# Gathering expert 0's rows turned, with the tokens as stationary operand, in a decoder layer with 32 experts

## What is computed

```python
def moe_ffn(h, w_router, b_router, w1, b1, w2, b2):
    logits = h @ w_router + b_router
    top_logit, top_e = lax.top_k(logits, 4)
    gate = softmax(top_logit)
    # for each expert e, over the tokens tok that chose it:
    #   u = h[tok] @ w1[e] + b1[e]          (1024 -> 2048: gate and linear half)
    #   y = clamped_swiglu(u) @ w2[e] + b2[e]   (1024 -> 1024)
    #   out[tok] += y * g

x = x + dot(concatenate([ret, moba]), w_out)
x = x + moe_ffn(rms_norm(x, norm2_w), ...)
out = rms_norm(x, final_norm_w)
```

## Time and profile before

| | |
|---|---|
| time, median of 3 runs | 1038.68 us (1038.46 to 1039.01) |
| the profiled execution: time, and its span from first to last instruction | 1039.17 us, 1037.3 us |
| PE busy | 1020.7 us (98%), 4880 matmul instructions |
| PEld, DVE, ACT busy | 409.8, 245.4, 126.5 us |
| mean granted PE clock | 0.997 |
| DMA | 424.64 MB, mean 409 GB/s |
| chain that ended last | PE 90%, DMA 7%, SPq 1% |

### The profile page before, as it was taken

One profiled execution on the slowest core, in us unless ns is written; L12 is line 12 of the kernel. 1 busy time (PEld: TensorE's weight loads), 2 busy tenths in 40 slices (PEclk: granted clock), 3 DMA queues, 4 the chain that ended last, 5 costly groups with the idle time before them and its releaser, 6 DMA issues.

```text
span 1037.3 us, 11270 instructions
## 1 busy us (share of the span) xinstructions
PE 1020.7 (98%) x4880; PEld 409.8 (40%) x4880; DVE 245.4 (24%) x610; ACT 126.5 (12%) x246; POOL 0.2 (0%) x4
## 2 busy tenths in 40 slices
PE   9999999999999999999999999999999999999996
PEld 8888433333333333333333333333333333333331
DVE  5776332111111111111111111111111111111111
ACT  2433120000000000000000000000000000000002
POOL 0000000000000000000000000000000000000000
PEclk9999999999999999999999999999999999999999
DMA  9983999999999999999999999999999999999995
GB/s 324 365 337 143 418 376 425 426 428 426 434 432 426 438 429 427 435 427 429 434 429 433 430 428 437 429 428 435 426 432 433 429 430 433 428 436 420 430 421 227
DMA packets 36104, 424.64 MB, mean 409 GB/s; under 512 B 3176, under 2 KB 16112, under 8 KB 19536
## 3 DMA queue, kind: packets, MB, share of 16 engines
q1 hardware_dynamic: 35744, 423.51, 97.0%
q10 hardware_dynamic: 304, 0.33, 0.1%
HBM read 422.78 MB, written 1.05 MB: 409 GB/s over the span
## 4 chain that ended last, share of the span: by engine, by line
PE 90%; DMA 7%; SPq 1%; DVE 0%; another core or an unknown queue 0%; issue 0%; ACT 0%; DVEq 0%
PE PS L1837 40%; PE PS L1860 19%; DMA ring<-in_w 7%; PE PS L1442 6%; PE PS L1806 5%; PE PS L1788 5%; PE PS L1685 3%; PE PS L1645 3%; PE PS L1895 2%; PE PS L1798 2%; PE PS L1411 1%; PE PS L1780 1%; SPq L543 1%; PE PS L1388 0%; PE PS L1968 0%; PE PS L1982 0%
## 5 line engine op out<-in xcount | busy, mean ns | idle before, releaser
L1837 PE MATMUL PS<-ring,work 128*64 128x512 f32 x1976 | 433.8, 596 | 6.0 <-DMA ring<-in_w 5.5
L1837 PEld LDWEIGHTS PS<-ring,work 128*64 128x64 f32 x1976 | 139.6, 137 | 277.2 <-issue 266.5
L1860 PE MATMUL PS<-ring,work 128*64 128x512 f32 x1024 | 227.9, 596 | 0.9 <-DMA ring<-in_w 0.8
L1860 PEld LDWEIGHTS PS<-ring,work 128*64 128x64 f32 x1024 | 72.0, 137 | 153.8 <-issue 148.9
L1300 DVE TENSOR_SCALAR work<-PS 128x512 f32<-128x512 f32 x32 | 22.1, 691 | 385.4 <-PE PS L1837 385.4
L841 ACT ACTIVATE work<-work 128x512 f32<-128x512 f32 x32 | 20.2, 631 | 523.5 <-DVE work L1300 523.5
L1265 DVE TENSOR_TENSOR work<-PS,n2w 128x512 f32<-128x512 f32 x30 | 20.7, 691 | 228.5 <-PE PS L1798 228.5
L1442 PE MATMUL PS<-ring 128*128 128x256 f32 x280 | 64.5, 382 | 0.0
L1806 PE MATMUL PS<-late,work 64*128 64x512 f32 x248 | 61.9, 616 | 0.0
L1788 PE MATMUL PS<-resid,work 128*64 128x512 f32 x248 | 58.5, 592 | 0.0
L1442 PEld LDWEIGHTS PS<-ring 128*128 128x128 f32 x280 | 51.7, 190 | 7.7 <-issue 1.4
(11 more groups left out here) (196 smaller groups left out, 453.2 us busy)
## 6 DMA issues: line engine op xcount, KB each, us to landing
ring<-in_w SPq DMA_DIRECT2D x72, 4096.0 KB, 34.8
ring<-in_w SPq DMA_DIRECT2D x35, 2048.0 KB, 13.5
ring<-in_w SPq DMA_DIRECT2D x22, 1024.0 KB, 8.4
ring<-in_w_in SPq DMA_DIRECT2D x11, 1024.0 KB, 12.1
ring<-in_w_out SPq DMA_DIRECT2D x4, 1024.0 KB, 11.1
ring<-in_w SPq DMA_DIRECT2D x6, 512.0 KB, 7.0
ring<-in_w_in SPq DMA_DIRECT2D x2, 512.0 KB, 5.8
work<-in_w SPq DMA_DIRECT2D x1, 768.0 KB, 8.2
```

The source lines that it names most:

```text
L1837: last = mm(bank(b0 + v)[64 * half:64 * half + 64, :], rows[:, c, :], turned_half(w[:, v * F:(v + 1) * F], half), start=(second and c == 0 ...
L1860: last = mm(out[64 * half:64 * half + 64, :], aT_n[:, c, 64 * h:64 * h + 64], ring[:, 2 * d + c // 2, cols:cols + BANK], start=(h == 0 and ...
```

## The change

Expert 0's gather is done the other way round: `x_cols(t, c)` is the stationary operand and `pick` the moving one, so that each matmul gives 128 features by 64 slots at once, in banks 5 and 3, summed over the two tiles. The copies into `gx` and the transposes go. The bias is done in one piece (`first_bias`) ahead of the wait for tile 1's `pick`. With `gx` unused at that time, the megabyte in `moved_w` is one DMA.

```diff
@@ SP
-            sp.dma_start(moved_w[:, BANK:], moved_src[:, BANK:]).then_inc(moved_in, 16)
-            sp.wait_ge(gather0_done, 2)
-            sp.dma_start(moved_w[:, 0:BANK], moved_src[:, 0:BANK]).then_inc(moved_end_in, 16)
+            sp.dma_start(moved_w, moved_src).then_inc(moved_in, 16)
@@ ACT
-            act.wait_ge(rows0_done, 1)
-            nc.scalar.activation(gx[0:64, :], bank(4)[0:64, :], ACT.Copy).then_inc(rows0a_ready, 1)
@@ DVE
-            dve.wait_ge(rows0_done, 2)
-            nc.vector.tensor_copy(gx[64:P, :], bank(4)[64:P, :]).then_inc(rows0b_ready, 1)
             take_gather0(0).then_inc(gh0_ready, 1)
@@ PE
+            def first_bias():
+
+                for v in range(2):
+                    for half in range(2):
+                        last = mm(bank(v)[64 * half:64 * half + 64, :], bsel0[v * E:(v + 1) * E, :],
+                                  turned_half(b1_sb[v * E:(v + 1) * E, :], half), start=True, stop=False)
+                return last
...
-            def gather0_rows(t, half):
-
-                return mm(bank(4)[64 * half:64 * half + 64, :], pick[:, t, :], resid[:, t, half_cols(half)],
-                          start=(t == 0), stop=(t == T - 1))
-
-            def turn_rows0(half):
-
-                rows = slice(64 * half, 64 * half + 64)
-                gx_v = gx.rearrange("p (i s) -> p s i", s=DEAL)
-                for c in range(4):
-                    last = nc.tensor.transpose(bank(TURN0_BANK[half])[:, c * SLOTS:(c + 1) * SLOTS], gx_v[rows, c, :],
-                                               ident[rows, rows])
-                last.then_inc(gather0_done, 1)
+            def gather0(t, half):
+
+                for c in range(4 * half, 4 * half + 4):
+                    at = (c % 4) * SLOTS
+                    last = mm(bank(TURN0_BANK[half])[:, at:at + SLOTS], x_cols(t, c), pick[:, t, :],
+                              start=(t == 0 and c % 4 == 0), stop=(t == T - 1), skip_group_check=True)
+                return last
...
             pe.wait_ge(pick0_ready, 1)
             for half in range(2):
-                gather0_rows(0, half)
+                gather0(0, half)
...
             pe.wait_ge(bsel_ready, 1)
-            bias_half(0, bsel0)
+            first_bias().then_inc(bias_done, 1)
             pe.wait_ge(pick_ready, 1)
             for half in range(2):
-                gather0_rows(1, half).then_inc(rows0_done, 1)
-            bias_half(1, bsel0).then_inc(bias_done, 1)
-            pe.wait_ge(rows0a_ready, 1)
-            turn_rows0(0)
-            pe.wait_ge(rows0b_ready, 1)
-            turn_rows0(1)
+                gather0(1, half).then_inc(gather0_done, 1)
...
                             pe.wait_ge(moved_in, 16)
-                            pe.wait_ge(moved_end_in, 16)
```

More of the change, by code:

```diff
@@ L313, in layer_kernel @@
         moved_in = sem("moved_in")
-        moved_end_in = sem("moved_end_in")
         ahead_in = sem("ahead_in")
@@ L399, in layer_kernel @@
         prefix0_done = sem("prefix0_done")
-        rows0_done = sem("rows0_done")
-        rows0a_ready = sem("rows0a_ready")
-        rows0b_ready = sem("rows0b_ready")
         gather0_done = sem("gather0_done")
```

## The result

The changed kernel takes 1045.5 us, median of 4 runs (1043.85 to 1046.43); the kernel before, run beside it, takes 1038.85 (4 runs, 1038.46 to 1039.3). The ratio is 1.0062, 95% interval 1.0045 to 1.0080: **0.6% slower**. The forecast was 1038.3 with a range up to 1040.3. The profiled execution is the fastest of the four, 1043.85 us with a span of 1042.1.

The account below looks back on a forecast made before the run. Bound: PE until expert 0 starts, then the weight stream. New stretch 1.92 + 0.20 + 1.02 + 1.92 + 0.30 = 5.36 us against 5.79, so 0.4 us earlier: span 1036.9, median 1038.3 us, range 1037.4 to 1040.3.

Parts of the forecast that it names:

- One for one: Whatever moves PE's start on expert 0 moves the ring loads, the moment the weight stream fills and the end equally.
- I take 0.12: Expert 0's new gather: each of 32 load-and-matmul pairs takes 0.12 us, so 1.92 us for each tile's 16.
- Break-even: Pair period in expert 0's gather at which the change gains nothing: 0.133 us.
- The row used as the nearest: Trace row of eight transposes with the same strided operand stationary, 0.12 us each, used to price the gather's pairs.
- The slow read mostly hides in the float32 load: In expert 0's gather, the strided read adds little to the load, whose period without stride is 0.11 us.
- Rival 2: Strided read sets the pace of the gather's float32 loads: +0.9 us at 0.16, +2.4 us at 0.21; chance 0.22.
- Rival 5: PE's clock falls to 0.50 beside expert 0: +1.3 us at the end, 1040.0; chance 0.03.
- The bias in front: Whole bias before tile 1's gather holds PE 1.02 us, its four small tiles side by side; bound 1.02 to 2.0.
- rival 3: Bias tiles pair up badly: 1.0 us more before the second gather, +0.6 us at the end, 1039.3; chance 0.04.
- Load and stream overlap: In the gather, a load overlaps with a running matmul though both use all 128 rows, so loads set the pace.
- What was removed, and the change-overs: Row gathers go, and 2.21 us after tile 1's gather; change-overs between tile shapes add 0.30 us for both gathers.
- The moved megabyte at 0: Sending the moved weights as one early DMA gains 0; up to 0.6 us if the 148 us hole weren't decisive.

## Why the prediction was wrong, point by point

- **What bounds the kernel: right.** The formula, stream full from a certain moment, gave 5.1 us from the bytes against 4.8 of span. "One for one" holds to within 0.8 us: in the profiles of the changed kernel (two), of 128 and 256 columns and of neighbouring columns, expert 0's first 32 matmuls ended 5.3, 6.0, 4.2, 4.3 and -0.7 us later than before, and the spans differ by 4.8, 5.9, 3.4, 4.6 and -1.0.
- **The term that failed: "I take 0.12", the period r of a load-and-matmul pair.** It was 3.81 / 16 = 0.238 us. Break-even had been put at 0.133. The 32 pairs took 32 x (0.238 - 0.12) = 3.8 us more than in the sum. The runs with 4, 8, 16 and 32 bytes show the stride as the cause, and those with 128 and 256 streamed columns that the load and not the streaming sets the pace.
- **Why the bounds did not hold it.** The row used as the nearest was that of a transpose, whose pace is 0.11 us without the stride and 0.12 with it, so it could not show what a slow load costs. The slower load in the earlier trace rows was no measure of it either: it isn't the same effect, since it is there at 8 bytes (0.208 us) as at 16 (0.209). In the float32 matmul the stride adds 0.329 - 0.192 = 0.137 us to a load and 0.238 - 0.113 = 0.125 us to a pair. So a row of the same operand under another kind of instruction was no bound, and 0.21 was no upper end. "The slow read mostly hides in the float32 load" was wrong: nearly all of it showed. Why the two kinds of instruction differ stays open. The estimate that was made by the rule of the Trainium skill, 0.18 us and 1.5 us slower than before, had the right sign and came nearer than the one that I took; the 0.07 us in it came from the transpose, so its size was luck.
- **Rival 2 (slower, by the stride) had the mechanism**, with chance 0.22, and its far end was too near. At r = 0.238 its own formula gives 32 x 0.105 = +3.4 us, which the runs without a fall of the clock bear out: 1042.57 - 1039.13 = +3.4 and 1042.87 - 1039.13 = +3.7 us.
- **Rival 5 (the clock falls) came on top**, at a chance of 0.03, and not by itself: slow loads leave PE little to stream. It made the bias 1.91 - 1.02 = 0.9 us longer and the first 32 matmuls of expert 0 8.32 - 7.09 = 1.2 us, together 2.1 us in the profiled execution. By the ratios it is 1.0062 or 1.0056 against 1.0035, 2.2 to 2.8 us, with intervals so wide that anything from a few tenths to 5 us would do. The prediction had priced the two as alternatives; they share a cause, so their costs add: 3.4 to 3.7 and the 2.1 of the trace make 5.5 to 5.8, and 6.65 was measured in the first set of runs and 5.8 in the second. The 0.9 to 1.2 us that are missing in the first set are within the intervals; a low clock that begins later and covers more of expert 0 would do it too.
- **The bias in front: right.** 1.02 us at full clock, in the new order of tiles; rival 3 is out.
- **Load and stream overlap: right**, shown for up to 256 columns.
- **What was removed, and the change-overs: right in size.** With r = 0.113 the stretch was 4.97 us; the sum would have given 32 x 0.113 + 0.20 + 1.02 + 0.30 = 5.14.
- **The moved megabyte at 0: not contradicted.** In neither pair of versions do one and two DMAs differ beyond the intervals. Whether there are some tenths in it stays open; so does what exactly sets the moment at which the clock falls.

## What to carry to other kernels

Before an operand goes to the stationary side, look at the distance between its elements: here 16 bytes or more between float32 columns doubled the time of a pair, 8 bytes cost 0.2 us over 32 pairs, and a better layout for one expert alone took the cost away. A price from another kind of instruction on the same operand is a hint, not a bound, and a pace in which the load doesn't show can't price the load. Two rivals with one cause are one case, with the sum of their prices.

## What the runs showed of the hardware that was not expected

- A float32 load of 128 x 128 for a matmul takes 0.192, 0.196, 0.329 and 0.335 us with 4, 8, 16 and 32 bytes between its elements. The cost is a step between 8 and 16 bytes. In a transpose the step lies elsewhere: 0.140 us at 4 bytes, 0.208 at 8, 0.209 at 16.
- The pace of slow loads doesn't follow PE's clock: 16 of them take 3.81 us at full clock (with 256 columns streamed) and 3.81 at half clock (the second gather of the changed kernel), whereas the bias went from 1.02 to 1.91.
- A stretch in which PE is shown as busy without a break can still lose its clock: with 64 columns streamed per strided load it fell to half for about 10 us, with 128 columns it stayed.
- The layout by twos, whose up weights come in runs of 16 KB instead of 32 KB on a partition and in another order, lowered a saturated weight stream from 430 to 428 GB/s, which is about 4 us over this kernel.
